# Five-layer network on one core: the second weight split of a layer moved behind its norm, the last stage's second input turned earlier, frequency tables regrouped

## The reference, cut to what matters

```python
def conv_gated_ffn(xn, w_up, conv_w, conv_b, w_down):        # ffn0 to ffn3
    h = causal_depthwise_conv(xn @ w_up, conv_w, conv_b)
    a, g = jnp.split(h, 2, axis=-1)
    return (jax.nn.silu(g) * a) @ w_down

# ffn4 and the last stage
gate, up = jnp.split(rms_norm(x, g_ffn) @ w_ffn_in, 2, axis=-1)
x = x + (jax.nn.silu(gate) * up) @ w_ffn_out
ple_gate = jax.nn.sigmoid(rms_norm(x, g_ple) @ w_ple_gate)
x = x + ple_gate * (p @ w_ple_proj)          # p: 256 x 256, does not depend on x
```

## Time and profile before

| what | us |
|---|---|
| median of 3 runs (1923.6 to 1924.94) | 1923.67 |
| the profiled execution, its own time | 1924.64 |
| its span | 1922.9 |
| TensorE busy | 1786.4 (93%) |
| VectorE busy | 1220.0 (63%) |
| ScalarE busy | 850.1 (44%) |
| GpSimd busy | 460.4 (24%) |

### The profile page before, as it was taken

How to read it: one execution, slowest core, us unless ns; L and a number is a source line. 1 busy time by engine, 2 the same in 40 slices (tenths; PEclk the granted TensorE clock), 3 DMA queues, 4 the chain that set the end, 5 groups by cost and what they waited for, 6 DMA issues and landing times.

```text
span 1922.9 us, 27465 instructions
## 1 busy us (share of the span) xinstructions
PE 1786.4 (93%) x11538; PEld 1583.5 (82%) x11538; DVE 1220.0 (63%) x1676; ACT 850.1 (44%) x1084; POOL 460.4 (24%) x641
## 2 busy tenths in 40 slices
PE   7999999989990998889999999999989999999997
PEld 7878999879980983448999888899988888899987
DVE  5556767567752779986666655566666556754444
ACT  5445455535540540015545444554543545444342
POOL 1210554148995027760000011200004100000000
PEclk9999999999995998899999999999989899999998
DMA  7434556445652551114555533555545521545550
GB/s 242 128 110 144 186 179 216 164 154 190 215 187 76 186 198 66 66 66 153 194 179 181 170 112 108 154 192 182 177 140 169 176 88 67 175 158 193 177 173 23
DMA packets 201530, 293.90 MB, mean 153 GB/s; under 512 B 6240, under 2 KB 162080, under 8 KB 199360
## 3 DMA queue, kind: packets, MB, share of 16 engines
q1 hardware_dynamic: 197568, 272.25, 42.9%
q0 software_dynamic: 2688, 11.51, 1.9%
q10 hardware_dynamic: 1152, 8.39, 1.2%
HBM read 282.70 MB, written 9.44 MB: 152 GB/s over the span
## 4 chain that ended last, share of the span: by engine, by line
PE 71%; DVE 13%; POOL 9%; ACT 4%; issue 2%; DMA 1%; SPq 0%; DVEq 0%; POOLq 0%; ACTq 0%
PE ps L108 70%; POOL arena L120 8%; DVE arena L120 3%; DVE arena L132 3%; DVE wlo L120 3%; ACT whi L114 2%; ACT arena L114 2%; DVE arena L126 1%; PE ps L111 1%; DVE arena L138 1%; DVE arena L123 1%; POOL sm L120 1%; DVE xres L120 1%; DVE arena L129 0%; DVE sm L123 0%
## 5 line engine op out<-in xcount | busy, mean ns | idle before, releaser
L120 DVE TENSOR_TENSOR wlo<-raw,whi 128x2048 fp32r<-128x2048 f32 x258 | 600.7, 2330 | 340.8 <-ACT whi L114 340.7
L108 PE MATMUL ps<-xh,whi 128*128 128x256 f32 x2288 | 654.8, 286 | 50.6 <-DVE wlo L120 49.1
L108 PE MATMUL ps<-xl,whi 128*128 128x256 f32 x2288 | 650.4, 284 | 0.0
L108 PE MATMUL ps<-xh,wlo 128*128 128x256 f32 x2288 | 650.4, 284 | 0.0
L114 ACT ACTIVATE whi<-raw 128x2048 fp32r<-128x2048 f32 x258 | 491.8, 1907 | 257.6 <-PE ps L108 237.7
L108 PEld LDWEIGHTS ps<-xh,whi 128*128 128x128 f32 x2288 | 441.6, 193 | 60.3 <-DVE wlo L120 49.4
L108 PEld LDWEIGHTS ps<-xl,whi 128*128 128x128 f32 x2288 | 441.8, 193 | 1.6
L108 PEld LDWEIGHTS ps<-xh,wlo 128*128 128x128 f32 x2288 | 441.6, 193 | 0.0
L108 PE MATMUL ps<-whi,oh 128*128 128x512 f32 (+1 forms) x640 | 251.6, 393 | 17.3 <-DVE ol L120 16.5
L120 POOL TENSOR_TENSOR arena<-arena 128x512 f32<-128x512 f32 (+4 forms) x250 | 230.2, 940 | 93.7 <-DVE arena L132 37.6
L108 PE MATMUL ps<-wlo,oh 128*128 128x512 f32 (+1 forms) x640 | 248.9, 389 | 0.0
(11 more groups left out here) (132 smaller groups left out, 1679.2 us busy)
## 6 DMA issues: line engine op xcount, KB each, us to landing
raw<-in_ffn_w_up SPq DMA_DIRECT2D x88, 1024.0 KB, 5.1
raw<-in_ffn_w_down SPq DMA_DIRECT2D x44, 1024.0 KB, 4.9
raw<-in_sb_w_qkv SPq DMA_DIRECT2D x24, 1024.0 KB, 5.2
raw<-in_w_ffn_in SPq DMA_DIRECT2D x22, 1024.0 KB, 5.1
raw<-in_w_in SPq DMA_DIRECT2D x19, 1024.0 KB, 5.1
raw<-in_w_ffn_out SPq DMA_DIRECT2D x11, 1024.0 KB, 4.8
raw<-in_sb_w_o SPq DMA_DIRECT2D x8, 1024.0 KB, 4.9
tabs<-arena POOLq DMA_DIRECT2D x8, 1024.0 KB, 4.6
```

Source lines behind the costliest of these rows:

```text
L108: return NOP if self.e is None else self.e.matmul(*a, **k)
L120: return NOP if self.e is None else self.e.tensor_tensor(*a, **k)
```

## The change

The last `cut_lo` before `add_residual` gets the distance 1 in place of 2 in all layers, so that the second tile of the next layer is split by that layer's first `cut_lo`, which stands behind `turned_dve` (in the last stage: ahead of it). Table 1 moves to ffn0, table 2 to gate, and 3 to 7 stay in ffn1. The turning and splitting of `p` moves into step 2 of ffn4, into slots 6 and 7 of `oh` and `ol`.

```diff
             if blk >= 2:
-                self.cut_lo(dv, ("dn", l, blk - 2))
+                self.cut_lo(dv, ("dn", l, blk - 2), 2 if blk < NB + 1 else 1)
...
-        self.cut_lo(dv, ("proj", st, 3))
+        self.cut_lo(dv, ("proj", st, 3), 1)
...
-        self.cut_lo(dv, ("proj", "gate", 3))
+        self.cut_lo(dv, ("proj", "gate", 3), 1)
...
-            self.cut_lo(dv, ("glu", hf, 0, 1))
+            self.cut_lo(dv, ("glu", hf, 0, 1), 2 - hf)
...
-            self.cut_lo(dv, ("proj", "second", i))
+            self.cut_lo(dv, ("proj", "second", i), 2 if i < 3 else 1)
...
+    def p_turn_pe(self, pe):
...
+            if blk == 2:
+                pe.wait_ge(*self.on("gated", 4, 1))
+                pe.wait_ge(*self.on("silu", 4, 1))
+                pe.wait_ge(*self.on("p_in"))
+                for kk in range(2):
+                    for t in range(2):
+                        ins = pe.transpose(b[:, kk * 256 + t * P:...], ps[:, t, kk * P:...], self.ident[:, :])
+                ins.then_inc(*self.up("p_turned"))
...
+    def p_turn_act(self, ac):        # blk 2: one copy of 128 x 512 to oh[6:8]
+    def p_turn_dve(self, dv):        # blk 2: one subtraction of 128 x 512 to ol[6:8], signal prep_out 4 2
...
     def ple_pe(self, pe):
-        (4 transposes of p to bank 0, signal p_turned)
         w = self.tile(pe, "pp")
-        pe.wait_ge(*self.on("ol", "p"))
-        self.tok_major(pe, w, 2, 0, 2, self.oh, self.ol, outs, 512).then_inc(*self.up("tile", "pp"))
+        self.tok_major(pe, w, 2, 0, 2, self.oh[:, 6:8, :], self.ol[:, 6:8, :], outs, 512).then_inc(*self.up("tile", "pp"))
...
-        (ple_act: wait for p_turned, 2 copies to oh; ple_dve: 2 subtractions to ol)
...
-        self.s5_tables_pool(po, range(0, 1))
+        self.s5_tables_pool(po, range(0, 2))
         self.rstd_pool(po, "gate")
         self.gating_pool(po)
-        self.s5_tables_pool(po, range(1, 2))
+        self.s5_tables_pool(po, range(2, 3))
         self.rstd_pool(po, "ffn1")
-        self.s5_tables_pool(po, range(2, 8))
+        self.s5_tables_pool(po, range(3, 8))
...
-PREP_BANKS = {(0, 3): 2, (1, 10): 9, (3, 5): 4}
+PREP_BANKS = {(0, 3): 2, (1, 10): 9, (3, 5): 4, (4, 3): 2}
```

More of the change, by code:

```diff
@@ L2290, in ple_bufs, with at @@
         return carve(self.ar, 512, 2, D), carve(self.ar, 2560, 2, D)
-    def ple_pe(self, pe):
[L2293 to L2298, removed]
+    def p_turn_pe(self, pe):
+        ps, b = self.nsa_views()["PS"], self.B[2]
+        def at(blk):
+            if blk == 2:
[4 more added lines that the diff above has]
+                    for t in range(2):
+                        ins = pe.transpose(b[:, kk * 256 + t * P:kk * 256 + (t + 1) * P], ps[:, t, kk * P:(kk + 1) * P], self.ident[:, :])
+                ins.then_inc(*self.up("p_turned"))
+        return at
+    def p_turn_act(self, ac):
+        def at(blk):
+            if blk == 2:
+                ac.wait_ge(*self.on("p_turned"))
+                ac.activation(self.oh[:, 6:8, :], self.B[2][:, :].rearrange("p (a b) -> p a b", b=256), ACT_F.Copy).then_inc(*self.up("oh", "p"))
+        return at
+    def p_turn_dve(self, dv):
+        def at(blk):
+            if blk == 2:
+                dv.wait_ge(*self.on("oh", "p"))
+                dv.tensor_tensor(self.ol[:, 6:8, :], self.B[2][:, :].rearrange("p (a b) -> p a b", b=256), self.oh[:, 6:8, :].bitcast(F32),
+                                 ALU.subtract).then_inc(*self.up("prep_out", 4, 2))
+        return at
+    def ple_pe(self, pe):
+        B = self.B
         w = self.tile(pe, "pp")
-        pe.wait_ge(*self.on("ol", "p"))
         outs = [[B[2 * t + j][:, :] for j in range(2)] for t in range(2)]
-        self.tok_major(pe, w, 2, 0, 2, self.oh, self.ol, outs, 512).then_inc(*self.up("tile", "pp"))
+        self.tok_major(pe, w, 2, 0, 2, self.oh[:, 6:8, :], self.ol[:, 6:8, :], outs, 512).then_inc(*self.up("tile", "pp"))
         self.norm_pe(pe, "ple")
@@ L2315, in ple_act @@
         B = self.B
[L2316 to L2319, removed]
         self.cut_hi(ac, ("pp",))
@@ L2333, in ple_dve @@
         pj, sg = self.ple_bufs()
[L2334 to L2337, removed]
         self.cut_lo(dv, ("pp",))
@@ L2413, in scalar @@
         self.norm_act(ac, "ffn4", 72)
-        self.ffn_act(ac, 4)
+        self.ffn_act(ac, 4, self.p_turn_act(ac))
         self.ple_act(ac)
@@ L2441, in vector @@
         self.turned_dve(dv, "ffn4", 72)
-        self.ffn_dve(dv, 4, "ple")
+        self.ffn_dve(dv, 4, "ple", self.p_turn_dve(dv))
         self.ple_dve(dv)
@@ L2465, in tensor @@
         self.norm_pe(pe, "ffn4")
-        self.ffn_pe(pe, 4)
+        self.ffn_pe(pe, 4, self.p_turn_pe(pe))
         self.ple_pe(pe)
-PREP_BANKS = {(0, 3): 2, (1, 10): 9, (3, 5): 4}
+PREP_BANKS = {(0, 3): 2, (1, 10): 9, (3, 5): 4, (4, 3): 2}
 def program(nc, A, out):
```

## The result

The changed kernel took 1890.91 us in the median of four runs (1889.54 to 1892.0), the kernel before 1923.91 beside it (1923.6 to 1924.94): a ratio of 0.9827 with a 95% interval of 0.9810 to 0.9844. The profiled execution took 1889.97, its span is 1887.8, the mean granted clock 0.973 against 0.961. Forecast were 1886.6 and 37.1 us less. 35.1 us went out of the span of the profiled execution; the medians of this comparison lie 33.0 us apart, those of experiment 4, the same pair again, 36.0.

The account below looks back on a forecast made before the run. TensorE, busy 1786.4 of 1922.9 us, was taken to starve behind GpSimd's tables in ffn1 and behind splits at layer ends. 18.7 + 10.7 + 8.3 - 0.6 = 37.1 us less gave 1886.6, range 1879 to 1897.

Parts of the forecast that it names:

- Part 1: ffn1: five tables in place of six behind the norm drop a fast one, shortening VectorE's standstill at b: -18.7 us.
- rival 1: ffn1: the table that falls out is worth a slow one, 32.65 us, standstill near 18: 1872.6 us, chance 0.07.
- rival 3: ffn1 and gate: something else holds step 7, or table 1 runs into gate's norm: 1905.3 us, chance 0.05.
- they take the same places in time: ffn1: the five remaining tables keep their times, so the last, a fast one of 18.69 us, falls out.
- the rule: End of ffn0: two-input VectorE and SBUF-reading GpSimd instructions exclude each other, so table 1 delays splits: up to 3 us less gain.
- Part 2: Nine layer ends: moving the second split lets the norm start sooner: -10.7 us, clock gains included.
- Seven gaps: Gaps ahead of seven norms, 1.05 to 2.28 us before, fall to 0.6 each: 7.9 us.
- s5's end: Gap at the end of s5, held more by the last product than the split: 0.3 us, between 0 and 1.7.
- the clock: Norms behind gaps of 0.6 us run at full clock, 2.4 GHz: 1.3 us, bounds 0 and 2.3.
- Rival 2: Layer starts: second splits come late because VectorE is busier behind a norm, giving 10.7 back: 1897.3 us, chance 0.11.
- Rival 4: Layer starts: the weight stream breaks if loads exceed 12.9 us; slower than before from 17.1, 1932.5 at 18; chance 0.03.
- Parts 3 and 4: Last stage: `pp` starts at once, gate tiles earlier, -8.3 us; ffn4: four transposes of `p` add 0.6 us.

Follow-up runs that it names:

- experiment 4: The changed kernel again, nothing edited, timed beside the kernel before: 1889.37 us, ratio 0.9817.
- experiment 6: The changed kernel without the making of table 7, its buffer stored as it is: 1878.1 us, ratio 0.975.
- `p` alone: The kernel before with only the turning and splitting of `p` moved into ffn4: 1913.25, 1914.77 and 1917.27 us, ratio 0.9946.
- tables alone: The kernel before with only the tables regrouped (0 and 1 in ffn0, 2 in gate, 3 to 7 in ffn1): 1908.71 us, ratio 0.9914.
- splits alone: The kernel before with only each layer's second weight split moved behind the norm: 1914.96 us, ratio 0.9946.
- experiments 9 and 11: 9: changed kernel, one of second's late splits ahead of its copies, 1890.1 us; 11: also ffn4's early split, `xl` first, ffn1's b at step 9, 1868.26 us.
- experiment 5: The changed kernel with the early second split kept in ffn4 and `xl` ahead of the last stage's own split: 1887.07 us, ratio 0.9804.
- experiment 8: The changed kernel with VectorE's work on b in ffn1 moved from step 7 to 8, on c from 8 to 10: 1880.36 us, ratio 0.9768.
- experiment 10: The changed kernel with VectorE's work on b in ffn1 moved from step 7 to 9, on c from 8 to 10: 1871.15 us, ratio 0.9725.

## Why the prediction was right, and where it was off

The sum came out within 2 us of the span, and the mechanism of each part was found in the traces. But single terms were off by as much as 3 us, in both directions, and that they nearly cancel is partly luck.

**Part 1** was mis-sized: 18.7 forecast, 17.1 measured in the changed kernel. The rest of its mechanism held: the tables bound the stretch (experiment 6), the last and fast one falls out (rival 1 is out: the standstill is 31.8, not near 18), the chain behind it is 14.04 as before, the first power isn't late (rival 3 is out). Alone the term is right, 30.4. What failed is the step "they take the same places in time", because part 2 changes one place. Time from the first clearing in ffn1 to the last store, in six traces:

| kernel | splits at layer ends | tables | us |
|---|---|---|---|
| before | early | 6 | 158.29 (438.70 to 596.99) |
| `p` alone | early | 6 | 158.30 (440.13 to 598.43) |
| tables alone | early | 5 | 139.61 (440.64 to 580.25) |
| splits alone | late | 6 | 159.87 (434.48 to 594.35) |
| changed | late | 5 | 141.17 (433.95 to 575.12) |
| changed, again | late | 5 | 141.17 (435.66 to 576.83) |

The table is worth 18.7 with early and with late splits; late splits cost the tables 1.6 us. The loss is in the first table behind the norm, which takes 29.4 us to its store in place of 24.5; the four behind it win 3.4 of these 4.9 back, and why isn't shown. What the first one meets shows in GpSimd and VectorE at ffn1's start, changed kernel:

```profile
438.13 5.16 POOL L120 TENSOR_TENSOR arena<-arena,p 128x128 f32<-128x128 f32 x2
443.38 0.60 POOL L120 TENSOR_TENSOR arena<-arena 128x64 f32<-128x64 f32 x2
444.06 3.23 POOL L120 TENSOR_TENSOR arena<-arena,p 128x256 f32<-128x256 f32 x2
```

```profile
438.55 4.48 DVE L120 TENSOR_TENSOR wlo<-raw,whi 128x2048 fp32r<-128x2048 f32 x2
...
444.24 2.58 DVE L120 TENSOR_TENSOR wlo<-raw,whi 128x2048 fp32r<-128x2048 f32 x1 [1.20 <-ACT whi L114]
```

and in GpSimd of the kernel before:

```profile
442.89 0.76 POOL L120 TENSOR_TENSOR arena<-arena,p 128x128 f32<-128x128 f32 x2
443.72 0.60 POOL L120 TENSOR_TENSOR arena<-arena 128x64 f32<-128x64 f32 x2
444.41 1.19 POOL L120 TENSOR_TENSOR arena<-arena,p 128x256 f32<-128x256 f32 x2
```

The same two multiplications take 5.16 us in place of 0.76 when two splits run back to back beside them: the next instruction of GpSimd starts 0.35 us behind the end of the splits. One thing is not parted: in the three traces with early splits the norm into ffn1 also ran at the low clock, and in the three with late ones at the full, so VectorE's `xl` and splits came sooner for this reason as well. The prediction cited the rule for this (the Trainium skill, "SBUF — State Buffer", "Who interferes with whom") and applied it to table 1 in ffn0, where the tables alone lost 0.8 us and the full change 0.3 (348.00 - 155.49 = 192.51 against 192.25 with the splits alone), well under its 3. The rule agrees with the rows above; where it cost most was a place at which the sum had put it nowhere.

**Part 2**, 10.7 forecast. Up to the norm into ffn4 the changed kernel gained 28.2, of which 17.1 are the tables: 11.1. The splits alone gave 10.4. Seven gaps are 0.5 (0.6 forecast), second's 3.27 (3.33), s5's end moved from 2.30 to 2.05 (0.3 forecast): together some 10.0 in place of 9.5. That the whole of 11.1 lies so near to the forecast is luck, since larger terms that the sum did not have cancel. The norms gained 3.9 by the clock in place of 1.3: the one into ffn2 0.9 and the one of second 1.6, which the sum had left at the old clock. Against that stand the wait at second's second tile, and 2.9 lost in second's attention (below).

Rival 2 had its mechanism at one place, the one named: the wait of 1.35 us at second's second tile. From the norm to the third tile it is 38.80 us, 38.91 before, so the wait took back what second's norm had won by the clock; by experiments 9 and 11 it costs 1.6 us with the norm at that clock. Two further waits for `wlo` stand inside second, 1.00 us at its third tile (0.99 before) and 1.79 at 1485.38. Rival 4 did not show: behind the first tiles of the kernel ScalarE never waits for `raw`, though one load took 12.6 us to land, near the 12.9 of its condition.

**The clock** came out better in the norms and worse elsewhere. Norms behind gaps of 0.5 us ran at full clock, as forecast. But in second's attention, which the change doesn't touch, the gain fell by 1.45 us twice (29.45 at 1524.24 before and 1494.79 after, 28.01 at 1545.15 and 1517.14, 26.56 at 1570.79 and 1544.23). Busy time and clock there, columns as in the earlier trace rows, after and then before:

```profile
1494.55:1500.55 6.00, 5.76 (x23) 5.12 (x24) 1.26 (x7) 2.79 (x5) 0.00 (x0) 0.50 0.78 247
1530.55:1536.55 6.00, 6.00 (x34) 5.35 (x34) 2.23 (x10) 2.65 (x6) 0.00 (x0) 0.58 0.00 0
```

```profile
1524.00:1530.00 6.00, 5.76 (x33) 5.26 (x33) 2.00 (x7) 2.78 (x5) 0.00 (x0) 0.72 0.78 247
1560.00:1566.00 6.00, 6.00 (x37) 5.60 (x37) 3.11 (x8) 3.20 (x6) 0.00 (x0) 0.74 0.00 0
```

The same code stays at 1.2 GHz for longer in this trace of the changed kernel. The second trace of the changed kernel passes the first of these sections in 19.42 us (1497.86 to 1517.28), where the first trace takes 22.35 and the kernel before 20.91; it lost its time ahead of second instead. All fourteen traces together say the same. From the norm of second to the one into ffn4 they take 251.5 to 256.6 us; the eleven with late splits lie at 251.5 to 252.8, but for the first trace of the changed kernel (256.0) and that of experiment 5 (256.05). So this term isn't one of the change: it moves by 3 to 4 us between executions of the same code, and the trace shown first had the bad case.

**Parts 3 and 4**, 7.7 forecast together (8.3 - 0.6). At the gate tiles they gained 7.75 (35.93 - 28.18); behind them 0.8 was lost, where 0.1 was forecast, in a longer stretch at 1.2 GHz behind a hole of 5.5 us (granted clock 0.55 over the first 6 us behind it, 0.72 before, behind one of 2.9). That two splits stand ahead of `xl` was foreseen; without that, 2.5 us more come out (experiment 5).

The sum: 17.1 + 11.1 + 7.75 - 0.8 = 35.1 (28.18 + 7.75 - 0.83), forecast 37.1. Another 0.4 us lies outside the span (2.17 of the profiled execution's time, 1.74 before).

## What to carry to other kernels

Look at an engine's load in the stretch that ends in a stall, not over the whole span: GpSimd was 24% busy overall but 112 of 118 us ahead of the stall, and its last table, with the loads queued behind it, set 49 us of TensorE's idle time. What helps is to place the consumer's wait as late as its own deadline allows and to put divisible work into the idle time ahead of a due time; together with the reordered last stage that brought 1861.79 us, 29 us more than the change. When two edits put work on two engines in the same few microseconds, price them together: a split that cost TensorE nothing at ffn1 was not free for GpSimd.

## What the runs showed of the hardware

- In these traces VectorE and GpSimd hold each other up by whole instructions, both ways: a pair of GpSimd multiplications of 0.76 us took 5.16 beside two back-to-back splits, and a VectorE instruction of 0.29 us took 1.91 behind a long GpSimd one. GpSimd did not get in between the two splits: its pair, begun at 438.13, ended at 443.29, the splits at 443.03. The last table took 18.69 us from store to store beside an idle VectorE (before), 19.61 with VectorE at work for the first 1.9 us (changed kernel), 25.76 with the first 13.4 (experiment 8) and 31.09 beside one at work throughout (experiment 10).
- After the same gap in the same code TensorE did not always do the same: behind 2.05 us ahead of the norm into ffn2 the norm ran at full clock in the first trace of the changed kernel (4.44 us with its inner wait) and at the lower one in the second (5.46), and second's attention stayed at the lower clock for different lengths of time. The eight executions of the changed kernel lie between 1888.56 and 1893.86 us; an effect of 3 us or less in one trace is to be checked in a second.
